# A chunked recurrence inside a decoder layer: its levels in turns of two chunks, with the projection work taken out from between them

## The reference

```python
def step(S, inp):
    r_t, w_t, k_t, v_t, a_t, b_t = inp
    sa = jnp.einsum('bhij,bhj->bhi', S, a_t)
    S = S * w_t[:, :, None, :] + sa[..., None] * b_t[:, :, None, :] + v_t[..., None] * k_t[:, :, None, :]
    y = jnp.einsum('bhij,bhj->bhi', S, r_t)
    return S, y
```

## Time and profile before

| | |
|---|---|
| median of 3 runs | 1158.3 us (1156.88 to 1160.41) |
| the profiled execution | 1164.61 us, span 1162.7 us |
| TensorE busy | 1087.3 us, 94% |
| VectorE, ScalarE, GpSimd busy | 549.1, 357.5, 501.8 us |
| mean granted TensorE clock | 0.975 |
| chain that ended last | PE 80%, DVE 10%, POOL 4%, waits without a cause shown 2% |
| recurrence | about 138 to 346 us |
| attention | about 454 to 650 us |

### The profile page before, as it was taken

One profiled execution on the slowest core, in us unless ns is written; L12 is line 12 of the kernel. 1 busy time (PEld: TensorE's weight loads), 2 busy tenths in 40 slices (PEclk: granted clock), 3 DMA queues, 4 the chain that ended last, 5 costly groups with the idle time before them and its releaser, 6 DMA issues.

```text
span 1162.7 us, 19062 instructions
## 1 busy us (share of the span) xinstructions
PE 1087.3 (94%) x7608; PEld 846.5 (73%) x7608; DVE 549.1 (47%) x910; ACT 357.5 (31%) x675; POOL 501.8 (43%) x431
## 2 busy tenths in 40 slices
PE   5998899989996899999998899999999999999996
PEld 3775577777775657666676677788888888888885
DVE  5786744463647162445444367234454454431113
ACT  4222212212110242444444344453322322322222
POOL 1444222221322644665578544743444444444442
PEclk9998899999998989999999999999999999999998
DMA  7343111100233524422111253732333333223231
GB/s 208 91 106 76 46 38 38 39 20 2 80 91 96 186 73 119 136 56 58 34 37 28 72 181 112 234 90 62 100 92 98 100 91 100 83 83 92 86 99 72
DMA packets 166046, 101.83 MB, mean 88 GB/s; under 512 B 21013, under 2 KB 154399, under 8 KB 165976
## 3 DMA queue, kind: packets, MB, share of 16 engines
q1 hardware_dynamic: 162336, 95.96, 28.7%
q10 hardware_dynamic: 3608, 4.88, 1.7%
q0 software_dynamic: 32, 0.00, 0.0%
HBM read 93.19 MB, written 7.63 MB: 87 GB/s over the span
## 4 chain that ended last, share of the span: by engine, by line
PE 80%; DVE 10%; POOL 4%; issue 2%; ACT 2%; DMA 1%; DVEq 0%; ACTq 0%; SPq 0%; POOLq 0%
PE ps L1481 20%; PE ps L1483 18%; PE ps L1482 18%; PE ps L1612 5%; PE ps L1525 3%; PE ps L1764 2%; PE ps L1811 2%; POOL WLO L564 2%; DVE XF L1231 1%; PE ps L1834 1%; PE ps L1836 1%; PE ps L1835 1%; DVE MT L1379 1%; POOL EB L625 1%; DMA PRAW<-in_par 1%
## 5 line engine op out<-in xcount | busy, mean ns | idle before, releaser
L564 POOL TENSOR_TENSOR WLO<-WRAW,WHI 128x1024 fp32r<-128x1024 f32 (+3 forms) x150 | 316.9, 2114 | 346.9 <-ACT WHI L926 197.0
L1481 PE MATMUL ps<-HHI,WHI 128*128 128x512 f32 x776 | 321.7, 415 | 18.1 <-DVE SQ L999 9.6
L1482 PE MATMUL ps<-HLO,WHI 128*128 128x512 f32 x776 | 305.9, 394 | 0.0
L1483 PE MATMUL ps<-HHI,WLO 128*128 128x512 f32 x776 | 305.9, 394 | 0.0
L1481 PEld LDWEIGHTS ps<-HHI,WHI 128*128 128x128 f32 x776 | 147.4, 190 | 75.5 <-issue 29.3
L1483 PEld LDWEIGHTS ps<-HHI,WLO 128*128 128x128 f32 x776 | 147.7, 190 | 32.3
L1482 PEld LDWEIGHTS ps<-HLO,WHI 128*128 128x128 f32 x776 | 147.9, 191 | 27.1 <-issue 1.0
L568 POOL CAST WHI<-WRAW 128x256 fp32r<-128x256 f32 (+1 forms) x83 | 49.0, 590 | 209.5 <-PE ps L1483 209.5
L926 ACT ACTIVATE WHI<-WRAW 128x1024 fp32r<-128x1024 f32 (+2 forms) x72 | 67.5, 937 | 140.0 <-PE ps L1483 140.0
L675 ACT ACTIVATE WHI<-WRAW 128x1024 fp32r<-128x1024 f32 (+1 forms) x55 | 47.8, 870 | 151.1 <-PE ps L1483 134.2
L1432 DVE TENSOR_TENSOR FT<-FT 128x512 f32<-128x512 f32 x22 | 50.9, 2313 | 89.0 <-ACT FT L932 89.0
(11 more groups left out here) (295 smaller groups left out, 1655.8 us busy)
## 6 DMA issues: line engine op xcount, KB each, us to landing
WRAW<-in_w_in SPq DMA_DIRECT2D x47, 512.0 KB, 4.0
WRAW<-in_w_gate SPq DMA_DIRECT2D x22, 512.0 KB, 3.9
WRAW<-in_w_up SPq DMA_DIRECT2D x22, 512.0 KB, 3.9
WRAW<-in_w_down SPq DMA_DIRECT2D x16, 384.0 KB, 3.5
spilled<-SQ SPq DMA_DIRECT2D x21, 256.0 KB, 2.3
WRAW<-in_w_down SPq DMA_DIRECT2D x16, 320.0 KB, 3.1
WRAW<-in_w_in SPq DMA_DIRECT2D x16, 256.0 KB, 3.5
WRAW<-in_w_branch SPq DMA_DIRECT2D x32, 128.0 KB, 2.8
```

The lines of the kernel that those rows point to most:

```text
L564: return pool.tensor_tensor(lo[:, 0:chunks, :], WRAW[:, n % NRAW, 0:chunks, :], hi[:, 0:chunks, :].bitcast(F32), ALU.subtract)
L1481: pe.matmul(dst, WHI[:, s, k, :], hi, start=start, stop=False)
L1482: pe.matmul(dst, WHI[:, s, k, :], lo, start=False, stop=False)
L1483: return pe.matmul(dst, WLO[:, s, k, :], hi, start=False, stop=stop)
```

## The change

In the recurrence each level is done in turns: the products of chunk 0's four slots, then of chunk 1's, each with its own semaphore count, eviction of 256 columns and place in PSUM: U in `R[c]` columns 0 to 255, XC in `R[c]` columns 256 to 511, XS in `R[2 + c]`. The fill between levels 1 and 5 is gone (10 steps a pair); 4 steps come between the first U and level 1, and 6 before it become 4. The products of values with G (`L1647`), the transposes and the scaling of `BK` come one to two levels later; T1 and SA change banks; TensorE waits for its own value products by `tv_mm`. VectorE's maskings are spread over other places. A pair has 19 steps of fill instead of 26 (22 instead of 29 in pair 1).

The table follows: 4 gate jobs fewer stand before the compressed branch (`NGA` 5 to 1), `PT_GN + 1` has 42 steps instead of 46, the first 39 attention iterations have 3 steps instead of 2, and the last one has 5 instead of 12.

```diff
-NGA = 5
+NGA = 1
-    PT_CP.append(len(FILL)); FILL += [5 if _cp == 0 else 2, 6] + [1, 1] * 5 + [1, 1, 1, 1, 4]
+    PT_CP.append(len(FILL)); FILL += [5 if _cp == 0 else 2, 4, 4] + [0] * 4 + [1, 1, 1, 1, 1, 4]
-PT_ATT = len(FILL); FILL += [2] * (NSA_STEPS + 3)
+PT_ATT = len(FILL); FILL += [3] * (NSA_STEPS + 3)
-FILL += [2 * (_rest // (2 * (NST - NSA_STEPS)))] * (NST - NSA_STEPS)
+FILL += [_rest // (NST - NSA_STEPS)] * (NST - NSA_STEPS)
...
@@ ScalarE
+                    for c in range(2):
+                        slots = slice(4 * c, 4 * c + 4)
+                        if lv < 5:
+                            act.wait_ge(xc_mm, 8 * cp + 2 * (lv - 1) + c + 1)
+                            act.activation(XC[:, slots, :], R[c][:, 256:512].rearrange("p (a b) -> p a b", a=4),
+                                           ACT.Copy).then_inc(xc_ok, 1)
+                        act.wait_ge(xs_mm, 10 * cp + 2 * (lv - 1) + c + 1)
+                        act.activation(XS[:, slots, :], R[2 + c][:, 0:256].rearrange("p (a b) -> p a b", a=4),
+                                       ACT.Copy).then_inc(xs_ok, 1)
...
@@ VectorE
+                    for c in range(2):
+                        dve.wait_ge(u_mm, 12 * cp + 2 * lv + c + 1)
+                        if lv > 1:
+                            dve.wait_ge(xs_mm, 10 * cp + 2 * (lv - 2) + c + 1)
+                        dve.tensor_tensor(UI[:, 4 * c:4 * c + 4, :], blocks(R[c][:, 0:256]), eyes, ALU.add).then_inc(ui_ok, 1)
                     if lv < 5:
                         am(lv + 1)
...
@@ TensorE
                 for lv in range(1, 6):
                     pe.wait_ge(am_ok, 6 * cp + lv + 1)
+                    for c in range(2):
+                        if lv == 1:
+                            pe.wait_ge(xc0_ok, 2 * cp + c + 1)
+                        else:
+                            pe.wait_ge(xc_ok, 8 * cp + 2 * (lv - 2) + c + 1)
+                        pairs(R[c][:, 0:256], c, AM[:, lv % 2, :, :], lambda p, j: XC[p, j, :]).then_inc(u_mm, 1)
+                    for c in range(2):
+                        pe.wait_ge(ui_ok, 10 * cp + 2 * (lv - 1) + c + 1)
...
+                        if lv < 5:
+                            pairs(R[c][:, 256:512], c, XS, lambda p, j: UI[p, j, :]).then_inc(xc_mm, 1)
+                        pairs(R[2 + c][:, 0:256], c, UI, lambda p, j: XS[p, j, :]).then_inc(xs_mm, 1)
```

More of the change, by code:

```diff
@@ L1606, in _, with pairs @@
                 fill(pt + 1)
-                def pairs(dst, lhsT, rhs):
-                    for j in range(NH):
+                def pairs(dst, c, lhsT, rhs):
+                    for m in range(4):
                         for p in half:
-                            last = pe.matmul(dst[p, j * C:(j + 1) * C], lhsT[p, j, :], rhs(p, j), start=True, stop=True)
+                            last = pe.matmul(dst[p, m * C:(m + 1) * C], lhsT[p, 4 * c + m, :], rhs(p, 4 * c + m), start=True, stop=True)
@@ new lines, in _ @@
+                    for c in range(2):
+                        if lv == 1:
[3 more added lines that the diff above has]
+                        pairs(R[c][:, 0:256], c, AM[:, lv % 2, :, :], lambda p, j: XC[p, j, :]).then_inc(u_mm, 1)
+                    for c in range(2):
+                        pe.wait_ge(ui_ok, 10 * cp + 2 * (lv - 1) + c + 1)
+                        if lv == 1:
+                            pe.wait_ge(x0_ok, cp + 1)
+                            pe.wait_ge(g_ok, 4 * cp + 2)
+                        else:
+                            pe.wait_ge(xs_ok, 10 * cp + 2 * (lv - 2) + c + 1)
+                        if lv < 5:
+                            pairs(R[c][:, 256:512], c, XS, lambda p, j: UI[p, j, :]).then_inc(xc_mm, 1)
+                        pairs(R[2 + c][:, 0:256], c, UI, lambda p, j: XS[p, j, :]).then_inc(xs_mm, 1)
@@ L1637, in _ @@
+                    if lv == 4:
                         pe.wait_ge(bkend_ok, cp + 1)
@@ L1642, in _ @@
                         last.then_inc(bkt_T, 1)
-                        for c in range(2):
-                            for m in range(4):
-                                for q in range(2):
-                                    h = 2 * m + q
-                                    pe.matmul(R[3][half[q], (4 * c + m) * C:(4 * c + m + 1) * C], G[64:128, c, 4 * q + m, 0:C],
-                                              SV[64:128, c, h * HD:(h + 1) * HD], start=c == 0 and m == 0, stop=False,
-                                              skip_group_check=True)
-                    fill(pt + 3 + 2 * (lv - 1))
+                for c in range(2):
+                    for m in range(4):
+                        for q in range(2):
+                            h = 2 * m + q
+                            last = pe.matmul(R[c][half[q], m * C:(m + 1) * C], G[64:128, c, 4 * q + m, 0:C],
+                                             SV[64:128, c, h * HD:(h + 1) * HD], start=m == 0, stop=False,
+                                             skip_group_check=True)
+                last.then_inc(tv_mm, 1)
+                fill(pt + 7)
+                pe.wait_ge(tv_mm, cp + 1)
                 pe.wait_ge(bkt_ok, 2 * cp + 2)
@@ L1656, in _ @@
                         for p in half:
-                            last = pe.matmul(R[3][p, (4 * c + m) * C:(4 * c + m + 1) * C], AR[p, m, c, 0:C], ST[p, g % 2, m, :],
+                            last = pe.matmul(R[c][p, m * C:(m + 1) * C], AR[p, m, c, 0:C], ST[p, g % 2, m, :],
                                              start=False, stop=True, skip_group_check=True)
@@ L1663, in _ @@
                                       start=m == 0, stop=False, skip_group_check=True)
-                    fill(pt + 12 + 2 * c)
+                    fill(pt + 8 + 2 * c)
                     pe.wait_ge(t1_ok, g + 1)
-                    pe.wait_ge(xs_ok, 5 * cp + 5)
+                    pe.wait_ge(xs_ok, 10 * cp + 10)
                     for m in range(4):
                         for q in range(2):
-                            last = pe.matmul(R[q][0:64, m * C:(m + 1) * C], XS[half[q], 4 * c + m, :], T1[half[q], c, m, :],
+                            last = pe.matmul(R[2 + q][0:64, m * C:(m + 1) * C], XS[half[q], 4 * c + m, :], T1[half[q], c, m, :],
                                              start=True, stop=True)
                     last.then_inc(sa_mm, 1)
-                    fill(pt + 13 + 2 * c)
+                    fill(pt + 9 + 2 * c)
                     pe.wait_ge(sa_dve, g + 1)
@@ L1688, in _ @@
                     values_T(cp + 1)
-                fill(pt + 16)
+                fill(pt + 12)
             fill(PT_GN)
```

70 lines of the change are left out of this document (22 added, 48 removed).

## The result

The changed kernel takes 1164.64 us (median of 8 runs, 1163.27 to 1170.52), the kernel before 1160.47 on the same chip (8 runs, 1156.88 to 1165.85): ratio 1.0051, 95% interval 1.0027 to 1.0075. It is slower by half a per cent. Forecast were 1161.0 us and "the same", in the range 1151 to 1174.

The account below looks back on a forecast made before the run. TensorE's stream plus its waits was taken to bound the kernel. Recurrence -7.9, after it +1.3 and attention +9.3 us sum to +2.7: 1158.3 to 1161.0 us as median, in the range 1151 to 1174.

Parts of the forecast that it names:

- the two big sums: Recurrence 7.9 us less with 1.3 more in the wait after it, and attention 9.3 us more.
- Levels: Recurrence levels: 3.25 us each with 0.17 of wait, gaining 4.2 us over 16 levels and 0.3 for level 5.
- Rival (b): TensorE's clock falls inside the recurrence levels: 1185 us, or 1173 if half of them; chance 0.09.
- Heads: Head of each pair, before level 1: 7.0 us, 4.6 less in all; masking gives 1.2 back, net 3.4.
- AR: Waits for AR ahead of the G products: 2.0 + 0 + 3.4 = 5.4 us, 1.5 more than before.
- Clock in the recurrence: Level 1 of pair 3: the 2.1 us wait goes and with it the low clock, 1.5 us gained.
- After the recurrence: TensorE's wait while VectorE prepares `XF`: 1.3 us more, lasting 10.5 to 12.5 us.
- The 1.4 that I took back: `XF` preparation: two conversions instead of three fall on it, so it ends 0.3 to 2.5 us sooner, taken as 1.4.
- Attention: Attention: five new waits 11.3 us, less 5.0 of old waits, plus 3.0 for the clock: 9.3 us more.
- The five waits: Attention iterations 2, 10, 18, 26, 34: jobs begin inside a fill and wait for GpSimd's piece, 11.3 us in all.
- Rival (a): Attention waits absent or half as long, clock stays: attention costs 1 to 3 us, 1153 us; chance 0.28.
- Rival (c): All five attention waits and the AR wait drop the clock: 6 us more, 1167 us; chance 0.20.

Follow-up runs that it names:

- e4: The changed kernel's tables with the old recurrence (no turns), fill taken out of its levels; 1189.3 us, ratio 1.0213 to the kernel before.
- e9: The new recurrence alone, attention steps as before, with two fill steps put back into each of levels 1 to 4; ratio 0.9980 to the kernel before.
- the second profile: The changed kernel profiled once more, unchanged; 1170.57 us.
- e1: The changed kernel with attention fills of 3, 3 and 2 steps in turn, so jobs begin with a fill; ratio 0.9924 to the kernel before.
- e6: The changed kernel with one more eviction in each half of the `XF` preparation after the recurrence; ratio 0.9991 to the kernel before.
- e5: The changed kernel with weights split ten steps ahead and projection jobs ending elsewhere in a pair; 1139.93 us, ratio 0.9812 to the kernel before.

## Why the prediction was right, and where it was off

The time and the sign of each stage came out, and the mechanism of the attention waits with them. The forecast of "no change" was 3.6 us short, just beyond the bound; 2.2 of these lie in the kernel before, whose median went from 1158.3 to 1160.5 with more runs, so the change itself is +4.2 us against +2.7. That the two big sums came out within 0.3 us each is partly luck: their terms missed by up to 2 us with opposite signs. Point by point:

- **Levels.** 3.07 to 3.12 us instead of 3.25, and 4.87 before. The gain is 0.4 us a level, 6.5 instead of 4.2 us, and e4 and e9 show that it needs the turns. The term mis-sized is "products of a level remain 3.08 us": issued in one row they take 2.95, and the wait is 0.13 (I took 0.17). Rival (b), that the clock falls in the levels, is false: 1.00 there. So the rule of the Trainium skill, TensorE: Matmul & The Clock Gate, section "A second HAM failure mode: psum-queue depth-cycling", does not show here: cycling through four banks with 0.13 us of wait a level left the clock alone. The price of the rival was too high as well: the 1.5 us were measured on a level of 4.9 us, so on 3.1 they are 0.95, and 16 levels cost 15 us, not 24.
- **Heads.** In pair 2 the head is 7.0 us, as said. No XC wait is left; in its place stand 0.31 us for AM in pair 1 and 0.79 for UI in pair 3, 1.1 where I had put 1.2 for masking, all of it in pair 3.
- **AR.** 1.96, 0 and 3.31: 5.3 against 5.4, by the place where the jobs end.
- **Clock in the recurrence.** I credited 1.5 us, since the wait of 2.1 goes. But the 3.31 wait that I had forecast myself was given no clock price. It dropped the clock (0.57), and the way from the G products to the U products was 6.51 instead of 4.98 us: 1.5 us, so this term is 0. In the second profile it did not, and the wait of 1.98 did; in e1, with both waits, neither did. A wait that a prediction adds must be charged as the one that it removes.
- **After the recurrence.** 12.29 us, in my bracket of 10.5 to 12.5, but 2.6 more instead of 1.3. Four steps less are 2.7. The 1.4 that I took back, since two conversions instead of three fall on `XF`, did come there: its preparation took 17.9 us instead of 20.3. But the third conversion falls on the four operations just ahead of it in VectorE's order (L1220), which took 5.20 instead of 2.73 us, and from the last update of the state on VectorE to the end of the wait it is 28.9 us before and 28.8 after. Recurrence and wait together: -6.9 us, forecast -6.6. About 1.1 of this is chance: in e1, which has the same recurrence, 50.8 us pass from the start of the stage to the G products of pair 2, in the changed kernel's profile 49.7.
- **Attention.** +9.6 us, forecast +9.3. The five waits are 10.3 us (11.3), by iteration 1.24, 1.73, 2.51, 2.19, 2.67 against 1.5, 1.9, 2.7, 2.3, 2.9; the old ones left are 1.1 (1.8). So the waits are 4.6 us more than before, where I had 6.3. The clock: I took two of five, 3.0 us; it is one of five in one execution, 1.6 us, and four of five in the other. The other 3.4 us of the 9.6 were not in the sum: 1.5 are the longer low clock at the start of the stage, and most of the other 1.9 is what a wait costs beyond its length. Rival (a) is false. Rival (c) is nearly what the slower group shows, 1170 instead of 1167: four of the five waits dropped the clock, and one AR wait.
- **What was missing:** that the clock behind these waits isn't a property of the kernel but of the execution. From the compressed scores to the merge the kernel before has only one wait above 1.6 us (3.07, at the merge), the changed kernel five. I had turned profile time into median by one fixed number, 6.3 us, from a profile of the higher group of before; for the changed kernel's profile, of the lower group, it is nearly 0.

## What to carry to other kernels

When steps of a background stream are handed out in another count per slot, look at where each unit of it begins inside a slot and how far ahead its inputs are prepared: a lead of one unit left waits of 6.2 to 6.8 us where units begin with slots and 11.4 where they don't, a lead of ten steps none. Two more steps of lead were worth 1.7% here, over three times what the change itself cost, and 0.7% in the kernel before. Judge a wait of 2 us on TensorE at its length plus about 1.5 us times the chance that the clock falls, and take two profiles before you compare spans that differ by less than 1%: the profile of e6, read against the wrong one of two, hides two thirds of its gain. When a helper engine slows a chain down, look not only at the collision but also at how much work the waiting engine has left when the chain begins.

## What the runs showed of the hardware

- Waits of 1.73, 2.20 and 2.51 us on TensorE, at the same place of the same program, were followed by the granted clock at 1.00 in one execution and by 0.61 to 0.66 in another; 2.67 dropped it in both. Longer waits are no surer: 3.31 us was followed by 0.57 in one execution and by 1.00 in the other, and 3.07 us, in the kernel before, by 1.00. What decides isn't known; the products and the waits are the same, and the wait of 1.73 ended at nearly the same time in both (461.66 and 462.10).
- A drop cost 1.4 to 1.6 us, and once 3.1.
- A wait of TensorE in attention cost 0.2 to 0.4 us more than its length, held product by product against the run without it.
- A VectorE operation of 128x504 with two SBUF inputs took 2.8 to 2.9 us beside a GpSimd subtraction, 0.67 us without one (before, after and e5). Moving the ends of the jobs didn't remove this in e5; TensorE only no longer waited for it.
